# First attention of a three-layer block: heads scored in pairs, one product for the gates' sums

## The chip, the core and the metric

The kernel runs on one core of one Trainium2 chip. A core has five engines that run side by side and wait for each other through semaphores: TensorE (matrix products; PE in the profile, PEld for its weight loads), VectorE (DVE), ScalarE (ACT), GpSimd (POOL) and SyncE (SP, which here starts most transfers). TensorE reads SBUF and writes PSUM, which has eight banks of 128 x 512 floats. The metric is the time of one execution on the device in microseconds (us).

## What is computed

A block of three layers on x of 256 tokens x 1024 channels. The first layer's mixer has a gated short convolution and, beside it, the attention with forget gates that this change is about. In it, eight heads of 64 channels are scored, and the running sums of the logarithms of their gates are added to the scores of the queries and taken from those of the keys:

```python
def forgetting_attention(q, k, v, logf):
    c = jnp.cumsum(logf, axis=1).transpose(0, 2, 1)
    for s0 in range(0, s_len, Q_BLOCK):                       # Q_BLOCK = 128
        logits = jnp.einsum("bqhd,bkhd->bhqk", q[:, s0:s1], k[:, :s1]) * scale
        logits = logits + c[:, :, s0:s1, None] - c[:, :, None, :s1]
        logits = jnp.where(kpos <= qpos, logits, -jnp.inf)
        p = jax.nn.softmax(logits, axis=-1)
        outs.append(jnp.einsum("bhqk,bkhd->bqhd", p, v[:, :s1]))
...
x = x + rmsnorm(mixer(rmsnorm(x)));  x = x + rmsnorm(swiglu(rmsnorm(x)))          # layer 1
# layers 2 and 3: block attention and differential attention, each with a feed-forward;
# their norms are modulated by silu(c) @ ada_w + ada_b (two matrices of 1024 x 6144)
```

## The kernel before

**Slabs.** Every weight comes as a slab of 128 x 2048 floats (1 MB). `load_order` (L88) writes the order of all slabs into STREAM: 160 main slabs in the order of their use, and between them 48 slabs of the modulation (ada). SyncE loads the stream into eight buffers in turn (`raw`, `sp_load` at L478), each as soon as its last user is done. ScalarE rounds a main slab to `high` (L490), VectorE makes the rest `low` (L496), and TensorE multiplies with both. Both engines do this three slabs ahead (AHEAD). An ada slab is used by VectorE alone: two sums of products of 128 x 1024 (L505). Where the ada slabs stand is set by the table `plan`: (count, first slab, last slab) for five stretches; before, 16 stand behind main slabs 4 to 22, and 9 in the first feed-forward.

**Slabs 4 to 14.** `pe_still` (L553) gives a slab of keys, queries, or the mixer's other inputs: 48 products of 256 columns (L569 to L571). Behind each of the slabs 4 to 14 stands one step of the attention, `pe_attend1(n)` with n from 0 to 10. Step n has up to three parts on TensorE: the values of head n-3 (L949, L950), the transposition of the probabilities of head n-2 (L910), and the scores of head n (L844, L962, L963). The scores of a head are, for each of the two query blocks (against 128 and against 256 keys), one product of queries and keys, then two products that take off the keys' sums of log gates, with `ck_hi` and `ck_lo` (the sums rounded, and the rest), each of eight rows, one per head, of which the stationary operand picks one.

**Shapes.** A product is on all 128 rows of the array, or on some: queries and keys of a head lie on 64 partitions (even heads on 0 to 63, odd ones on 64 to 127), the sums on eight. The values of a head have 64 columns of output partitions. The profile shows this as rows*columns ahead of the shape: 128*128, 64*128, 8*128, 128*64.

**VectorE and ScalarE in step n.** VectorE adds the mask and the queries' sums to the scores and finds their maximum (`dve_biased`, L857, L868); ScalarE takes the exponential after the rounding of the next slab (L878); VectorE divides after its next slab (`dve_weigh`, L885, L889); step n+2 transposes. Both engines carry the convolution of the mixer in the same steps. Each engine does its work strictly in the order in which it is written.

**PSUM.** Slabs, transpositions and scores take banks 0 to 3 in turn (`bank`): each waits until what was there is read. Values go to bank 4 + head pair.

The sums of log gates are made once, by L1143 (for the queries) and L1146 (for the keys, negative), from `logf` and `nlogf`, after slab 3; ScalarE copies them to `ck_hi` (L1263), VectorE makes `ck_lo` (L1437), and the first scores wait for that.

Of the kernel before, what the change touches and what calls it, by code (L numbers as in the profile page):

```python
# [12 lines left out]
P = 128  # L13
# [4 lines left out]
H = 8  # L18
# [18 lines left out]
for _name, _n in (("mix_pre", KC), ("ffn_pre", KC), ("conv", 3 * AC), ("subln", 1), ("b_f", NT * H), ("lam", 4 * DIFF)):  # L37
    COLUMNS[_name] = (sum(w for _, w in COLUMNS.values()), _n)
N_COLUMNS = sum(w for _, w in COLUMNS.values())

# [47 lines left out]
def load_order():  # L88

    nets = [(NUM["gate_up1", 0], NUM["moba_v", 0]), (NUM["gate_up2", 0], NUM["diff_v", 0]), (NUM["gate_up2", 2 * FG], len(MAIN))]  # L90
    plan = [(16, 4, 22), (9, nets[0][0] + 4, nets[0][0] + 24), (8, nets[0][1] + 4, nets[1][0] - 2),
# [72 lines left out]
def build_program(nc, dram, out):  # L164
    with ExitStack() as ctx:
# [40 lines left out]
        gate_f = sb("gate_f", [P, 5, NT * H])  # L206
        c_q = sb("c_q", [P, NT * H])
        ck_hi = sb("ck_hi", [H, S], F32R)
        ck_lo = sb("ck_lo", [H, S], F32R)
        ident_r = sb("ident_r", [H, H], F32R)  # L210
# [47 lines left out]
        u_f, a_f, l_f, logf, nlogf = (gate_f[:, i, :] for i in range(5))  # L258
# [572 lines left out]
        def prob_free(tag, h, i):  # L831
            if tag == "s1":
                return (turned, ("s1", h - 4)) if h >= 4 else (small_pe, "gates") if h == 3 else None
# [7 lines left out]
        def pe_scores(tag, h, i, q, k, more=None):  # L841
            o = yield from bank((tag, h, i), (biased, (tag, h, i)))
# [95 lines left out]

        def pe_attend1(n):
            if 0 <= n - 3 < H:  # L940
                h = n - 3
                rows = slice((h % 2) * HD1, (h % 2 + 1) * HD1)
                if h % 2 == 0:
                    yield from bank(("values", "s1", h // 2), *y_bank("s1", h // 2), at=4 + h // 2)
                yield from pe.wait_ge(probs_copied, ("s1", h))
                yield from pe.wait_ge(evacuated, ("values", "v1", 1, 0))
                o, p = psum[4 + h // 2], prob_t[h % 2]
                v = lambda c: work_v[:, c, h * HD1:(h + 1) * HD1]
                nc.tensor.matmul(o[rows, 0:S], v(0), p[:, 0:S], start=True, stop=False)  # L949
                nc.tensor.matmul(o[rows, P:S], v(1), p[:, S:3 * P], start=False, stop=True).then_inc(*applied.up(("s1", h)))  # L950
            if 0 <= n - 2 < H:
                yield from pe_turn_probs("s1", n - 2)
            if n < H:
                h = n
                part = slice((h % 2) * HD1, (h % 2 + 1) * HD1)
                yield from pe.wait_ge(evacuated, ("q1", h // 4))
# [3 lines left out]
                def minus_c(o, w):  # L960
                    row = ident_r[:, h:h + 1].to_broadcast([H, P])
                    nc.tensor.matmul(o, row, ck_hi[:, w], start=False, stop=False)  # L962
                    return nc.tensor.matmul(o, row, ck_lo[:, w], start=False, stop=True)  # L963

                yield from pe_scores("s1", h, 0, qT[part, h // 2, :], kT[part, h // 2, :], minus_c)

        def act_attend1(n):
            if 0 <= n - 3 < H and n % 2 == 0:
                k = (n - 3) // 2
                yield from act_y_hi("s1", k, applied, ("s1", n - 3), psum[4 + k][:, 0:S])  # L970
# [5 lines left out]
        def dve_attend1(n):  # L976
            if 0 <= n - 3 < H and n % 2 == 0:
                yield from dve_y_lo("s1", (n - 3) // 2, psum[4 + (n - 3) // 2][:, 0:S])
# [123 lines left out]
        def tensor():  # L1102
# [42 lines left out]
            for c in range(NT):  # L1145
                m = nc.tensor.matmul(o[0:H, S + c * P:2 * S], nlogf[:, c * H:(c + 1) * H], tri[:, 0:S - c * P],  # L1146
# [73 lines left out]
        def scalar():  # L1220
# [41 lines left out]
            nc.scalar.activation(ident_r[:, :], ident[0:H, 0:H], ACT.Copy)  # L1262
            nc.scalar.activation(ck_hi[:, :], psum[bank_of["sums"]][0:H, S:2 * S], ACT.Copy).then_inc(*small_act.up("ck"))  # L1263
# [16 lines left out]
            for g in range(2):  # L1280
                yield from act_next("mix", g)
# [394 lines left out]
```

## Time and profile before

| | us |
|---|---|
| median of 3 runs (1002.17 to 1004.49) | 1002.32 |
| the profiled execution's own time | 1003.79 |
| its span in the trace | 1002.4 |
| PE busy / DVE busy / ACT busy | 980.0 / 727.0 / 530.8 |
| granted clock of TensorE, mean | 0.995 |

The span runs from the first to the last instruction that the trace shows; the own time holds 1.39 us more. A busy time counts the stretches in which at least one instruction of the engine runs; products overlap, so that a product's duration is longer than the distance to the next. For TensorE the distances between starts are to be read, not the durations.

### The profile page before, as it was taken

To read this page: it belongs to the slowest core of one execution; us is meant where nothing else is said; L and a number is where in the kernel's file an instruction comes from. 1 tells how busy PE (TensorE), PEld (TensorE's weight loads), DVE (VectorE), ACT (ScalarE), POOL (GpSimd) and SP (SyncE) were. 2 spreads that over 40 slices of the span, in tenths; PEclk is the share of its full clock that TensorE was granted. 3 is DMA by queue.
4 is the path that set the end of the run, shared out by engine and by line. 5 is a ranking of instruction groups with operands and counts; after the bars stand their busy time and mean duration, and the time that the engine had idled before them with its cause. 6 is when DMAs were issued, how large, how long until landed. Compare 5 with 4: busy or idle time off the path is not lost.

```text
span 1002.4 us, 14063 instructions
## 1 busy us (share of the span) xinstructions
PE 980.0 (98%) x5762; PEld 856.4 (85%) x5762; DVE 727.0 (73%) x1102; ACT 530.8 (53%) x808; POOL 35.4 (4%) x58
## 2 busy tenths in 40 slices
PE   7999999999999999999999999999999899999997
PEld 7988899878888888899878888887997778888886
DVE  4798867778776777787777878777576768766573
ACT  5644435455444555565564554555567665545451
POOL 2000000011000000000000000001000000000000
PEclk8999999999999999999999999999999999999999
DMA  9665679546997764676467677764733246658511
GB/s 369 263 252 210 235 267 371 219 162 219 241 348 280 271 232 147 218 297 242 168 257 285 259 290 257 288 216 162 229 132 124 85 175 245 216 206 277 205 42 43
DMA packets 33441, 225.67 MB, mean 225 GB/s; under 512 B 4090, under 2 KB 4373, under 8 KB 7008
## 3 DMA queue, kind: packets, MB, share of 16 engines
q1 hardware_dynamic: 31104, 218.94, 60.1%
q0 software_dynamic: 1696, 5.08, 1.6%
q8 instruction: 46, 0.75, 0.3%
q10 hardware_dynamic: 576, 0.74, 0.2%
q14 instruction: 19, 0.16, 0.0%
HBM read 223.49 MB, written 1.26 MB: 224 GB/s over the span
## 4 chain that ended last, share of the span: by engine, by line
PE 85%; DVE 8%; ACT 5%; issue 1%; DMA 1%; POOL 0%; ACTq 0%; DVEq 0%
PE psum L586 20%; PE psum L588 10%; PE psum L625 8%; PE psum L626 8%; PE psum L627 8%; PE psum L569 7%; PE psum L570 7%; PE psum L571 7%; DVE low L496 4%; ACT high L490 2%; PE psum L844 2%; PE psum L694 1%; PE psum L696 1%; PE psum L695 1%; PE psum L311 1%
## 5 line engine op out<-in xcount | busy, mean ns | idle before, releaser
L496 DVE TENSOR_TENSOR low<-raw,high 128x2048 fp32r<-128x2048 f32 (+1 forms) x160 | 361.5, 2276 | 123.2 <-ACT high L490 122.8
L490 ACT ACTIVATE high<-raw 128x2048 fp32r<-128x2048 f32 (+1 forms) x160 | 299.4, 1897 | 36.0 <-DMA raw<-in_mix 9.4
L586 PE MATMUL psum<-h_both,high 128*128 128x512 f32 x960 | 239.9, 392 | 0.0
L586 PEld LDWEIGHTS psum<-h_both,high 128*128 128x128 f32 x960 | 174.3, 189 | 32.9 <-issue 0.5
L569 PE MATMUL psum<-h_both,high 128*128 128x256 f32 x544 | 156.6, 288 | 0.0
L570 PE MATMUL psum<-h_both,high 128*128 128x256 f32 x544 | 153.9, 283 | 0.0
L571 PE MATMUL psum<-h_both,low 128*128 128x256 f32 x544 | 153.9, 283 | 0.0
L588 PEld LDWEIGHTS psum<-h_both,low 128*128 128x128 f32 x960 | 131.0, 190 | 9.4
L588 PE MATMUL psum<-h_both,low 128*128 128x256 f32 x960 | 133.9, 282 | 0.0
L625 PE MATMUL psum<-high,y_hi 128*128 128x512 f32 x328 | 129.2, 394 | 2.6 <-DVE y_lo L932 1.7
L626 PE MATMUL psum<-low,y_hi 128*128 128x512 f32 x328 | 128.0, 390 | 0.0
L627 PE MATMUL psum<-high,y_lo 128*128 128x512 f32 x328 | 127.7, 389 | 0.0
L505 DVE CUSTOM_DVE_ANT_0 raw<-raw,c_row 128x1024 f32<-128x1024 f32 x96 | 113.5, 1220 | 1.0 <-DMA raw<-in_ada 1.0
L595 ACT ACTIVATE work_v<-psum 128x256 f32<-128x256 f32 x120 | 44.0, 376 | 119.6 <-PE psum L588 119.6
L569 PEld LDWEIGHTS psum<-h_both,high 128*128 128x128 f32 x544 | 104.2, 192 | 3.0 <-issue 1.7
L570 PEld LDWEIGHTS psum<-h_both,high 128*128 128x128 f32 x544 | 104.3, 192 | 0.2
L571 PEld LDWEIGHTS psum<-h_both,low 128*128 128x128 f32 x544 | 104.3, 192 | 0.0
L625 PEld LDWEIGHTS psum<-high,y_hi 128*128 128x128 f32 x328 | 61.7, 188 | 15.6 <-DVE low L496 1.9
L627 PEld LDWEIGHTS psum<-high,y_lo 128*128 128x128 f32 x328 | 61.6, 188 | 13.2
L626 PEld LDWEIGHTS psum<-low,y_hi 128*128 128x128 f32 x328 | 61.7, 188 | 11.5
L601 DVE TENSOR_TENSOR work_v<-psum,work_v 128x256 f32<-128x256 f32 x120 | 47.4, 419 | 20.8 <-ACT work_v L595 19.9
L764 ACT ACTIVATE y_hi<-work_v 128x512 fp32r<-128x512 f32 x30 | 19.0, 632 | 62.0 <-DVE work_v L787 62.0
(176 smaller groups left out, 1033.4 us busy)
## 6 DMA issues: line engine op xcount, KB each, us to landing
raw<-in_gate_up SPq DMA_DIRECT2D x66, 1024.0 KB, 5.6
raw<-in_ada SPq DMA_DIRECT2D x48, 1024.0 KB, 4.9
raw<-in_down SPq DMA_DIRECT2D x33, 1024.0 KB, 5.7
raw<-in_mix SPq DMA_DIRECT2D x14, 1024.0 KB, 6.9
raw<-in_moba_qk SPq DMA_DIRECT2D x8, 1024.0 KB, 6.0
raw<-in_diff_qk SPq DMA_DIRECT2D x8, 1024.0 KB, 4.9
raw<-in_qk SPq DMA_DIRECT2D x4, 1024.0 KB, 14.6
raw<-in_branch SPq DMA_DIRECT2D x4, 1024.0 KB, 5.8
```

Source lines behind the costliest of these rows:

```text
L490: nc.scalar.activation(high[n % N_HI][:, s], raw[i % N_RAW][:, s], ACT.Copy).then_inc(*rounded.up(n if key is None else key))
L496: nc.vector.tensor_tensor(low[i % N_RAW][:, s], raw[i % N_RAW][:, s], high[n % N_HI][:, s].bitcast(F32), ALU.subtract).then_inc(*rest.up(key))
L505: last = nc.vector.tensor_tensor_reduce(out=w, in0=w, in1=c_row[:, :], scale=1.0, scalar=0.0, op0=ALU.mult, op1=ALU.add, accum_out=mod_raw ...
L569: nc.tensor.matmul(to, a, hi(k), start=first, stop=False)
L570: nc.tensor.matmul(to, a, lo(k), start=False, stop=False)
L571: m = nc.tensor.matmul(to, r, hi(k), start=False, stop=last and j > j0)
L586: nc.tensor.matmul(o[:, :], wh[:, k, j * P:(j + 1) * P], h_both[:, k, :, :], start=k == 0, stop=False)
L588: m = nc.tensor.matmul(o[:, 0:S], wl[:, k, j * P:(j + 1) * P], h_hi[:, k, :], start=False, stop=k == KC - 1)
L601: nc.vector.tensor_tensor(place[:, j, :], psum[bank_of[*key, j]][:, 0:S], place[:, j, :], ALU.add).then_inc(*joined.up((*key, j)))
L625: nc.tensor.matmul(psum[b][:, :], hi(k0 + k, t), vh, start=first, stop=False)
L626: nc.tensor.matmul(psum[b][:, :], hi(k0 + k, t), vl, start=False, stop=False)
L627: m = nc.tensor.matmul(psum[b][:, :], lo(k0 + k, t), vh, start=False, stop=last)
```

## The change

It does four things. (1) The keys' sums come out of one product on all partitions: `nlogf` is now 128 columns wide with the eight heads at columns 0, 32, 64 and 96, and zeros between them. In the new tile `ck`, rows 0 to 7 and 64 to 71 hold the rounded sums, rows 32 to 39 and 96 to 103 the rest; one product of forty rows (`CK_ROWS`) replaces the two of eight, with a stationary operand (`pick`) that picks the head's row in both groups. (2) Even steps score two heads one behind the other, the odd one into bank 7; odd steps score none. (3) The values of two heads are made one behind the other in even steps from step 4 on. (4) The plan puts 14 ada slabs instead of 16 behind the slabs 4 to 22, and 11 instead of 9 into the first feed-forward. In steps 6 and 7 ScalarE and VectorE do the attention's part ahead of the convolution's last part.

```diff
-    plan = [(16, 4, 22), (9, nets[0][0] + 4, nets[0][0] + 24), (8, nets[0][1] + 4, nets[1][0] - 2),
+    plan = [(14, 4, 22), (11, nets[0][0] + 4, nets[0][0] + 24), (8, nets[0][1] + 4, nets[1][0] - 2),
...
+        nlogf = prob[2][:, 0:NT * P].rearrange("p (t n) -> p t n", t=NT)
...
-        def pe_scores(tag, h, i, q, k, more=None):
-            o = yield from bank((tag, h, i), (biased, (tag, h, i)))
+        def pe_scores(tag, h, i, q, k, more=None, at=None):
+            o = yield from bank((tag, h, i), (biased, (tag, h, i)), at=at)
...
         def pe_attend1(n):
-            if 0 <= n - 3 < H:
-                h = n - 3
...
+            if n % 2 == 0 and 0 <= n - 4 < H:
+                k = (n - 4) // 2
+                o = yield from bank(("values", "s1", k), *y_bank("s1", k), at=4 + k)
                 yield from pe.wait_ge(evacuated, ("values", "v1", 1, 0))
+                for h in (n - 4, n - 3):
+                    rows, p = slice((h % 2) * HD1, (h % 2 + 1) * HD1), prob_t[h % 2]
+                    yield from pe.wait_ge(probs_copied, ("s1", h))
...
-            if n < H:
-                h = n
+            for h in (n, n + 1) if n % 2 == 0 and n < H else ():
                 part = slice((h % 2) * HD1, (h % 2 + 1) * HD1)
+                sums = slice((h % 2) * HD1, (h % 2) * HD1 + CK_ROWS)
...
                 def minus_c(o, w):
-                    row = ident_r[:, h:h + 1].to_broadcast([H, P])
-                    nc.tensor.matmul(o, row, ck_hi[:, w], start=False, stop=False)
-                    return nc.tensor.matmul(o, row, ck_lo[:, w], start=False, stop=True)
-
-                yield from pe_scores("s1", h, 0, qT[part, h // 2, :], kT[part, h // 2, :], minus_c)
+                    return nc.tensor.matmul(o, pick[sums, h:h + 1].to_broadcast([CK_ROWS, P]), ck[sums, w], start=False, stop=True)
+
+                yield from pe_scores("s1", h, 0, qT[part, h // 2, :], kT[part, h // 2, :], minus_c, at=7 if h % 2 else None)
...
-                m = nc.tensor.matmul(o[0:H, S + c * P:2 * S], nlogf[:, c * H:(c + 1) * H], tri[:, 0:S - c * P],
+                m = nc.tensor.matmul(o[:, S + c * P:2 * S], nlogf[:, c, :], tri[:, 0:S - c * P],
...
-            nc.vector.tensor_scalar(nlogf, logf, -1.0, None, ALU.mult).then_inc(*small_dve.up("logf"))
+            yield from dve.wait_ge(small_pool, "blank")
+            for a in range(0, P, 32):
+                m = nc.vector.tensor_scalar(nlogf[:, :, a:a + H], logf.rearrange("p (t h) -> p t h", t=NT), -1.0, None, ALU.mult)
...
-            nc.vector.tensor_tensor(ck_lo[:, :], psum[bank_of["sums"]][0:H, S:2 * S], ck_hi[:, :].bitcast(F32), ALU.subtract).then_inc(
-                *small_dve.up("ck"))
+            for row in (32, 96):
+                rows = slice(row, row + H)
+                m = nc.vector.tensor_tensor(ck[rows, :], psum[bank_of["sums"]][rows, S:2 * S], ck[rows, :].bitcast(F32), ALU.subtract)
+            m.then_inc(*small_dve.up("ck"))
...
+            nc.gpsimd.memset(nlogf, 0.0).then_inc(*small_pool.up("blank"))
```

On TensorE, step 4 (behind slab 8) read before as follows. psum and a number is a bank, prob_t the transposed probabilities, high a rounded slab.

```order
L949 MATMUL psum4<-prob_t1,work_v 64x256 [waits probs_copied]
L950 MATMUL psum4<-prob_t1,work_v 64x128
L910 MATMUL psum3<-const,prob2 128x128 [waits weighted,produced]
L910 MATMUL psum3<-const,prob2 128x128 x2
L844 MATMUL psum0<-work 128x128
L962 MATMUL psum0<-ck_hi,ident_r 128x128
L963 MATMUL psum0<-ck_lo,ident_r 128x128
L844 MATMUL psum0<-work 128x256
L962 MATMUL psum0<-ck_hi,ident_r 128x256
L963 MATMUL psum0<-ck_lo,ident_r 128x256
L569 MATMUL psum1<-h_both,high3 128x256 [waits biased,rest]
```

After the change it reads so (the lines are three further down in the file; two more rows, L847 and L964 of 256 columns into psum7, follow):

```order
L952 MATMUL psum4<-prob_t0,work_v 64x256
L953 MATMUL psum4<-prob_t0,work_v 64x128
L952 MATMUL psum4<-prob_t1,work_v 64x256 [waits probs_copied]
L953 MATMUL psum4<-prob_t1,work_v 64x128
L913 MATMUL psum1<-const,prob2 128x128 [waits weighted,biased]
L913 MATMUL psum1<-const,prob2 128x128 x2
L847 MATMUL psum2<-work 128x128 [waits produced]
L964 MATMUL psum2<-ck,pick 128x128
L847 MATMUL psum2<-work 128x256
L964 MATMUL psum2<-ck,pick 128x256
L847 MATMUL psum7<-work 128x128 [waits biased]
L964 MATMUL psum7<-ck,pick 128x128
```

The values of heads 0 and 1 now stand together, and so do the scores of heads 4 and 5, of which the second waits on its own for bank 7. The products of eight rows are gone. Step 5, behind slab 9, has the transposition alone:

```order
L574 MATMUL psum3<-h_both,low5 128x256
L913 MATMUL psum0<-const,prob3 128x128 [waits weighted,evacuated]
L913 MATMUL psum0<-const,prob3 128x128 x2
L572 MATMUL psum1<-h_both,high4 128x256 [waits probs_copied,rest]
L573 MATMUL psum1<-h_both,high4 128x256
```

It has lost its values and its scores; they stand in steps 6 and 4. On SyncE, in the first feed-forward, before the change:

```order
L484 DMA raw0<-in_down1 128x2048
L484 DMA raw1<-in_ada 128x2048
L484 DMA raw2<-in_gate_up1 128x2048
L484 DMA raw3<-in_gate_up1 128x2048
L484 DMA raw4<-in_ada 128x2048
L484 DMA raw5<-in_down1 128x2048
L484 DMA raw6<-in_gate_up1 128x2048
L484 DMA raw7<-in_gate_up1 128x2048
L484 DMA raw0<-in_ada 128x2048
L484 DMA raw1<-in_down1 128x2048
L484 DMA raw2<-in_gate_up1 128x2048
L484 DMA raw3<-in_ada 128x2048
```

The same place after it:

```order
L487 DMA raw6<-in_down1 128x2048
L487 DMA raw7<-in_ada 128x2048
L487 DMA raw0<-in_gate_up1 128x2048
L487 DMA raw1<-in_gate_up1 128x2048
L487 DMA raw2<-in_ada 128x2048
L487 DMA raw3<-in_down1 128x2048
L487 DMA raw4<-in_gate_up1 128x2048
L487 DMA raw5<-in_ada 128x2048
L487 DMA raw6<-in_gate_up1 128x2048
L487 DMA raw7<-in_down1 128x2048
L487 DMA raw0<-in_ada 128x2048
L487 DMA raw1<-in_gate_up1 128x2048
```

The third ada slab comes one main slab earlier, since eleven now stand where nine stood.

## Rows read from the trace of the kernel before

**Rows 1.** The page: busy time of TensorE; the chain that ended last, by engine.
```profile
PE 980.0 (98%) x5762; PEld 856.4 (85%) x5762; DVE 727.0 (73%) x1102; ACT 530.8 (53%) x808; POOL 35.4 (4%) x58
...
PE 85%; DVE 8%; ACT 5%; issue 1%; DMA 1%; POOL 0%; ACTq 0%; DVEq 0%
```

**Rows 2.** Windows: us, busy time (x instructions) of PE, PEld, DVE, ACT, POOL, clock, DMA share, GB/s.
```profile
44.90:134.60 89.70, 89.70 (x650) 79.46 (x649) 74.80 (x132) 40.42 (x69) 0.00 (x0) 1.00 0.62 234
134.60:180.60 46.00, 46.00 (x384) 46.00 (x384) 34.96 (x37) 20.29 (x15) 0.00 (x0) 1.00 0.84 320
240.00:300.00 60.00, 60.00 (x319) 51.72 (x318) 44.81 (x54) 29.30 (x32) 5.72 (x10) 1.00 0.95 287
```

**Rows 3.** Timeline of PE, the step before slab 9: start us, us, engine, line, tiles, shape.
```profile
83.32 0.28 PE L571 MATMUL psum<-h_both,low 128*128 128x256 f32 x1
83.53 0.65 PE L949 MATMUL psum<-prob_t,work_v 128*64 128x256 f32 x2
84.01 0.38 PE L950 MATMUL psum<-prob_t,work_v 128*64 128x128 f32 x2
84.33 0.55 PE L910 MATMUL psum<-const,prob 128*128 128x128 f32 x3
84.80 0.48 PE L844 MATMUL psum<-work 64*128 64x128 f32 x2
85.22 0.32 PE L962 MATMUL psum<-ck_hi,ident_r 8*128 8x128 f32 x1
85.58 0.70 PE L844 MATMUL psum<-work 64*128 64x256 f32 x2
86.20 0.38 PE L962 MATMUL psum<-ck_hi,ident_r 8*128 8x256 f32 x1
86.43 0.28 PE L963 MATMUL psum<-ck_lo,ident_r 8*128 8x256 f32 x1
86.64 0.38 PE L569 MATMUL psum<-h_both,high 128*128 128x256 f32 x1
```

**Rows 4.** Timeline of PE, first product of slabs 4, 5, 6, 7, 8 and 15.
```profile
44.90 0.39 PE L569 MATMUL psum<-h_both,high 128*128 128x256 f32 x1
...
52.67 0.38 PE L569 MATMUL psum<-h_both,high 128*128 128x256 f32 x1
...
60.44 0.39 PE L569 MATMUL psum<-h_both,high 128*128 128x256 f32 x1
...
68.55 0.38 PE L569 MATMUL psum<-h_both,high 128*128 128x256 f32 x1
...
77.59 0.39 PE L569 MATMUL psum<-h_both,high 128*128 128x256 f32 x1
...
134.55 0.39 PE L569 MATMUL psum<-h_both,high 128*128 128x256 f32 x1
```

**Rows 5.** Timeline of PE, third attention, both halves of a head.
```profile
722.58 0.28 PE L571 MATMUL psum<-h_both,low 128*128 128x256 f32 x1
722.78 0.93 PE L844 MATMUL psum<-work 64*128 64x128 f32 x8
723.65 0.38 PE L569 MATMUL psum<-h_both,high 128*128 128x256 f32 x1
```

**Rows 6.** Timeline of DVE, then of PE, around the first score.
```profile
49.87 0.41 DVE L1437 TENSOR_TENSOR ck_lo<-psum,ck_hi 8x256 fp32r<-8x256 f32 x1 [0.54 <-ACT ck_hi L1263]
...
50.84 0.48 PE L844 MATMUL psum<-work 64*128 64x128 f32 x2
```

**Rows 7.** Timeline of DVE: a score's bias, with the wait before it.
```profile
77.70 0.74 DVE L857 SCALAR_TENSOR_TENSOR prob<-psum,c_q,const 128x128 f32<-128x128 f32 x2 [2.41 <-PE psum L963]
```

**Rows 8.** Timeline of DVE, then of PE: one slab of the first feed-forward.
```profile
288.61 2.29 DVE L496 TENSOR_TENSOR low<-raw,high 128x2048 fp32r<-128x2048 f32 x1 [1.02 <-ACT high L490]
...
298.00 0.63 PE L586 MATMUL psum<-h_both,high 128*128 128x512 f32 x2
```

**Rows 9.** The page, groups of instructions: busy us, mean ns; idle before, its releaser.
```profile
L505 DVE CUSTOM_DVE_ANT_0 raw<-raw,c_row 128x1024 f32<-128x1024 f32 x96 | 113.5, 1220 | 1.0 <-DMA raw<-in_ada 1.0
```

More of the change, by code:

```diff
@@ L257, in build_program @@
         table, hot = prob[0][0:BUCKETS + 1, 0:H * COPIES], prob[1][0:BUCKETS + 1, :]
-        u_f, a_f, l_f, logf, nlogf = (gate_f[:, i, :] for i in range(5))
+        u_f, a_f, l_f, logf = (gate_f[:, i, :] for i in range(4))
+        nlogf = prob[2][:, 0:NT * P].rearrange("p (t n) -> p t n", t=NT)
         def col(name, a=0, n=None):
@@ L832, in prob_free @@
             if tag == "s1":
[L833 removed]
+                return (turned, ("s1", h - 4)) if h >= 4 else (None, None, (small_pe, "sums"), (small_pe, "gates"))[h]
             if tag == "moba":
@@ L939, in pe_attend1 @@
         def pe_attend1(n):
-            if 0 <= n - 3 < H:
-                h = n - 3
[L942 to L945, printed above, removed]
-                yield from pe.wait_ge(evacuated, ("values", "v1", 1, 0))
[L947 to L950, printed above, removed]
+            if n % 2 == 0 and 0 <= n - 4 < H:
+                k = (n - 4) // 2
+                o = yield from bank(("values", "s1", k), *y_bank("s1", k), at=4 + k)
+                yield from pe.wait_ge(evacuated, ("values", "v1", 1, 0))
+                for h in (n - 4, n - 3):
+                    rows, p = slice((h % 2) * HD1, (h % 2 + 1) * HD1), prob_t[h % 2]
+                    yield from pe.wait_ge(probs_copied, ("s1", h))
+                    v = lambda c: work_v[:, c, h * HD1:(h + 1) * HD1]
+                    nc.tensor.matmul(o[rows, 0:S], v(0), p[:, 0:S], start=True, stop=False)
+                    nc.tensor.matmul(o[rows, P:S], v(1), p[:, S:3 * P], start=False, stop=True).then_inc(*applied.up(("s1", h)))
             if 0 <= n - 2 < H:
                 yield from pe_turn_probs("s1", n - 2)
-            if n < H:
-                h = n
+            for h in (n, n + 1) if n % 2 == 0 and n < H else ():
                 part = slice((h % 2) * HD1, (h % 2 + 1) * HD1)
+                sums = slice((h % 2) * HD1, (h % 2) * HD1 + CK_ROWS)
                 yield from pe.wait_ge(evacuated, ("q1", h // 4))
@@ L976, in dve_attend1 @@
         def dve_attend1(n):
-            if 0 <= n - 3 < H and n % 2 == 0:
-                yield from dve_y_lo("s1", (n - 3) // 2, psum[4 + (n - 3) // 2][:, 0:S])
+            if n % 2 == 0 and 0 <= n - 4 < H:
+                yield from dve_y_lo("s1", (n - 4) // 2, psum[4 + (n - 4) // 2][:, 0:S])
             if n < H:
@@ L1281, in scalar @@
                 yield from act_next("mix", g)
+                yield from act_attend1(6 + g)
                 yield from act.wait_ge(produced, ("conv", g))
@@ L1284, in scalar @@
                     *hi_made.up(("conv", g)))
-                yield from act_attend1(6 + g)
             for n, place in enumerate((gate_c, gate_a)):
@@ L1467, in vector @@
                     *produced.up(("conv", g)))
+                yield from dve_attend1(6 + g)
                 yield from dve.wait_ge(hi_made, ("conv", g))
@@ L1470, in vector @@
                     *lo_made.up(("conv", g)))
-                yield from dve_attend1(6 + g)
             for n in range(2):
@@ L1641 @@
         "lam": np.broadcast_to(a["diff_lambda_2"][0].reshape(1, -1), (P, 4 * DIFF)),
+        "pick": (row % 32 == np.arange(H)[None, :]).astype(np.float32),
     }
```

19 lines of the change are left out of this document (10 added, 9 removed).

## The prediction

> **What bounds the kernel now.** I read the page first, then the chain of waits, the windows of the attention, TensorE's timeline within one step, and last VectorE's timeline. The page shows TensorE busy for 980.0 us and on 85% of the chain that ended last, the other engines on 8% or less [rows 1]. In the window of steps 0 to 10, from slab 4 to slab 15, it is busy for all of 89.70 us, VectorE for 74.80 and ScalarE for 40.42 [rows 2]. So time saved on TensorE there ends the stretch earlier, as long as VectorE keeps up.
>
> The reader is to see in the next rows where TensorE's time goes though it looks busy. In the window without attention (134.6 to 180.6) 384 products of slabs take 46.00 us [rows 2], so 0.12 us each and 48 x 0.12 = 5.75 us a slab. Slab 4 begins at 44.90 and slab 15 at 134.55 [rows 4]: 89.65 us for eleven slabs (63.25) and eleven steps, which leaves 26.4 us for the attention. Step 0 is scores alone: 52.67 - 44.90 - 5.75 = 2.02 us. Step 2 is scores and a transposition: 68.55 - 60.44 - 5.75 = 2.36, so a transposition costs 0.34. Step 4 (slab 8 begins at 77.59, slab 9 at 86.64 [rows 3, 4]) has values too: 3.30, so values cost 0.94. Eight of each: 16.2 + 2.7 + 7.5 = 26.4, as measured.
>
> Most of a head's 2.02 us is no streaming. At each change of the rows or columns in use the next start is 0.2 us away: the slab's last product at 83.32, the values at 83.53; the sums' last product at 86.43, the next slab at 86.64 [rows 3]. Within a slab the distance is 0.12. A switch thus costs some 0.09 ahead of the new shape and as much behind it, where its first weights load uncovered. The scores of a head change shape five times: 128 to 64 rows, to 8 (85.22), to 64 (85.58), to 8 (86.20), to 128 (86.64).
>
> The nearest thing to the new pair stands in the third attention, where the two halves of a head lie on partitions 0 to 63 and 64 to 127, go to two banks, and have no product for sums between. Their eight records take from 722.78 to 723.65 [rows 5], 0.87 us. One after the other they could not: a 128-key record streams in about 0.11 (three transpositions in 0.34) and a 256-key one in 0.21 (0.48 from 83.53 to 84.01 for two, less the first load [rows 3]), which makes 4 x 0.11 + 4 x 0.21 = 1.28 without any load or switch. So the two halves run side by side although the program has one half behind the other. TensorE: Matmul & The Clock Gate, in the Trainium skill (Part 3, The mechanism), says that products start and end strictly in program order. By it the second head's streaming would come behind the first's; the trace disagrees, with 0.87 against at least 1.28, and its rule is rival B below.
>
> **The change part by part.**
>
> *Scores.* If forty rows count as the same half of the array as sixty-four, a pair is one visit: 0.09 + 0.87 + 0.09 = 1.05 us for queries and keys, plus two products for the sums per head, side by side with the other head's. Each costs at least nothing (under a load) and at most 0.36, what the two products and their switch take now (85.22 to 85.58 [rows 3]). I take 0.12 each, as a slab's product, since it has the same columns: 1.05 + 0.24 = 1.29. Before, two heads cost 2 x 2.02 = 4.04. Saved: 4 x 2.75 = 11.0 us. With the sums' products free it is 12.0.
>
> *Values.* Eight visits of 0.94 become four. If two heads on different columns run side by side too, a visit stays at 0.96, and 7.5 - 3.8 = 3.7 us go. No row shows two products on different columns at a time. If they don't, the second head adds its streaming, some 0.65 of the 0.80 between 83.53 and 84.33 [rows 3]: 4 x 1.59 = 6.4, and 1.2 us go. I take the first, because the rows of the array do it. TensorEngine Tiling (Array Packing), in the Trainium skill (Key Properties), says that tiles work independently and in parallel; by it too the saving would be 3.7, and no run here shows it for columns.
>
> *Transpositions.* As many as before, 0.34 each; in odd steps they stand between slabs of their own shape. Nothing.
>
> *Making the sums.* Once: four products with 128 stationary columns instead of eight. Four longer loads against two switches that go: between 0.2 us gained and 0.2 lost; taken at nothing. On VectorE `ck` needs a second subtraction, 0.41 long, behind one that starts at 49.87, so it is ready at about 50.65 instead of 50.28; the first score starts at 50.84 [rows 6]. That is a cover of 0.2 us; if it fails I lose 0.1 to 0.3. The three more negations, some 0.17 each by the smallest VectorE work here, and GpSimd's clearing of `nlogf` at the very start are ahead of a slab's worth of time; nothing.
>
> *VectorE.* Its work in the stretch is 74.80 us and its room falls from 89.7 to 75.0. It gets one ada slab less there (two sums of 1.22 [rows 9]) and 0.6 us of new work: 73 of 75. That is close, and it is the cover on which everything hangs. What keeps it from the path: it is ahead today, waiting 2.41 us for the scores of head 3 [rows 7], a rest is made three slabs ahead, and a division has a whole slab of 5.75 us until its transposition. An even step now waits for the odd head's bias two slabs before. Queued behind such a wait are the pair's scores and the next slab. I put 0.3 us for it, and 3 at worst.
>
> *Loads.* Two ada slabs move into the first feed-forward, where the DMA engines are busy for 95% of the time at 287 GB/s [rows 2], so 3.7 us per slab. A rest there ends at 290.90 and its slab starts at about 298.0 [rows 8], 7.1 us ahead. One or two slabs more in front of it leave 3.4 us or just nothing; the cost is between 0 and 2 us, taken at 0. In the first stage there are two slabs fewer in less time.
>
> Sum: -11.0 - 3.7 + 0.3 = -14.4 us. Against the profiled execution's own 1003.79 us that gives 989.4. It was 1.47 above the median of the runs, so the median should come to 987.9, say 988.0.
>
> **The rivals.**
>
> A. *Columns one after the other.* The values save 1.2 instead of 3.7: 11.0 + 1.2 - 0.3 = 11.9, 990.4 us. For it: no row shows columns together, and both heads write one bank. Against it: the rows do.
>
> B. *Heads in program order.* The second head's scores stream behind the first's: 0.64 + 0.24 = 0.88 more for a pair, 7.5 us saved instead of 11.0, and the values as in A: 993.9 (with the values side by side 991.4). Against it: [rows 5].
>
> C. *The cover fails in part.* VectorE at 73 of 75 us is late for banks or divisions, or the feed-forward's slabs come late: 1 to 3 us back, 989 to 991.
>
> D. *Forty rows are a shape of their own.* Then each head keeps its five switches and the halves can't overlap. Per head only two products of about 0.06 and 0.12 go, and per pair one switch to and from: 4 x (0.36 + 0.18) = 2.2, with the values' 3.7 less 0.3: 996.8. Against it: a head's array rows come in halves in every row that I have, and forty fit the half; but no row shows forty.
>
> E. *Slower, by VectorE.* In each of the four even steps with scores TensorE stands until VectorE has read the odd head's scores of two steps before. That costs nothing until VectorE is more than a slab late. It loses when the stand is over 3.6 us a step (14.4 / 4), and over 0.3% slower from 4.4 us a step: 1006 or more. For it: 97% load. Against it: VectorE's own work doesn't grow, and before it fitted with 14.9 us to spare.
>
> **How the numbers follow.** The forecast (986.5 to 989.5) has 0.50, A 0.20, C 0.14, B 0.08, D 0.05, E 0.03. The low end is the forecast with the sums' products free and 0.2 gained in making the sums, with some spread of the runs: 986.0. The high end takes in A, C and B's better half: 992.5. Left out are most of B, D and E above, and little below. A measurement of this kernel can't tell less than 0.3% (3 us) from no change; all cases but E are beyond that, with D nearest. So 0.95 faster, 0.02 the same, 0.03 slower.
>
> **What would show it.** On TensorE's timeline a pair's twelve records must begin within about 0.9 us, with distances of 0.01 to 0.02 between the two heads, and the next slab start 1.1 after the first. The even step from 4 on must take about 2.6 us, odd ones 0.34, and the stretch from slab 4 to slab 15 about 75. Gaps of 0.2 around the products of `ck` would be D, the second head's records behind the first's B, the same at L952 A. Waits of TensorE for VectorE in the stretch (there are none now) would be C or E. The forecast is wrong if the stretch shrinks by less than 12 us, or if it does and the end comes later by less: then the feed-forward has eaten it.

## The result and the profile after

| | before | after |
|---|---|---|
| median (4 runs each, one comparison) | 1002.25 (1001.91 to 1004.49) | 990.01 (989.59 to 990.60) |
| profiled execution's own time / span | 1003.79 / 1002.4 | 989.94 / 988.6 |
| slab 4 to slab 15 | 89.65 | 76.37 |

The ratio is 0.9873, 95% interval 0.9861 to 0.9885: faster by 1.3%, 12.2 us between the medians. The forecast was 988.0 us in a range of 986.0 to 992.5. The page of the changed kernel, busy time and chain by engine:

```profile
PE 966.1 (98%) x5746; PEld 849.7 (86%) x5746; DVE 727.4 (74%) x1106; ACT 531.0 (54%) x808; POOL 35.7 (4%) x59
...
PE 83%; DVE 9%; ACT 5%; issue 1%; DMA 1%; POOL 0%; ACTq 0%; DVEq 0%
```

TensorE is busy 13.9 us less than in [rows 1], the other engines as long as before. The windows that answer to [rows 2] (the attention, the slabs without it, the feed-forward):

```profile
44.41:120.81 76.40, 76.25 (x636) 72.77 (x634) 72.68 (x129) 40.49 (x69) 0.00 (x0) 1.00 0.69 261
120.81:166.86 46.05, 46.05 (x386) 46.05 (x385) 32.69 (x32) 20.27 (x15) 0.00 (x0) 1.00 0.79 298
226.20:286.20 60.00, 60.00 (x319) 51.72 (x318) 46.85 (x60) 29.09 (x32) 5.72 (x10) 1.00 0.97 304
```

The attention's window is 13.3 us shorter (it starts 0.03 ahead of slab 4's first product; the expectations below give the stretch as its 76.40), TensorE is busy in nearly all of it, and VectorE does nearly its old work in less room. The next two windows are full, as before. Behind the start of slab 15 the two executions take the same, 1002.4 - 134.55 = 867.85 us and 988.6 - 120.81 = 867.79: nothing was given back. The timeline of PE, first products of slabs 4, 5, 7, 8, 9 and 15, beside [rows 4]:

```profile
44.44 0.36 PE L572 MATMUL psum<-h_both,high 128*128 128x256 f32 x1
...
51.97 0.39 PE L572 MATMUL psum<-h_both,high 128*128 128x256 f32 x1
...
65.42 0.38 PE L572 MATMUL psum<-h_both,high 128*128 128x256 f32 x1
...
71.52 0.36 PE L572 MATMUL psum<-h_both,high 128*128 128x256 f32 x1
...
80.14 0.38 PE L572 MATMUL psum<-h_both,high 128*128 128x256 f32 x1
...
120.81 0.39 PE L572 MATMUL psum<-h_both,high 128*128 128x256 f32 x1
```

Less 5.75 us a slab, step 0 is 51.97 - 44.44 - 5.75 = 1.78 us (forecast 1.29) and step 2, behind an empty step 1, 65.42 - 51.97 - 11.5 = 1.95 (forecast 1.63). Step 3, a transposition alone, is 71.52 - 65.42 - 5.75 = 0.35, and step 4 is 80.14 - 71.52 - 5.75 = 2.87 (forecast 2.6). The timeline of PE in step 4 answers to [rows 3]:

```profile
77.45 0.66 PE L952 MATMUL psum<-prob_t,work_v 128*64 128x256 f32 x4
77.93 0.40 PE L953 MATMUL psum<-prob_t,work_v 128*64 128x128 f32 x4
78.25 0.55 PE L913 MATMUL psum<-const,prob 128*128 128x128 f32 x3
78.73 0.49 PE L847 MATMUL psum<-work 64*128 64x128 f32 x2
78.97 0.30 PE L964 MATMUL psum<-ck,pick 40*128 40x128 f32 x1
79.06 0.48 PE L847 MATMUL psum<-work 64*128 64x128 f32 x3
...
79.41 0.46 PE L964 MATMUL psum<-ck,pick 40*128 40x256 f32 x1
...
79.74 0.47 PE L964 MATMUL psum<-ck,pick 40*128 40x256 f32 x1
```

Three things are to be seen. The values of two heads, twice the records, take from 77.45 to 78.25, the 0.80 that one head took from 83.53 to 84.33 [rows 3]. At the sums' product there is no gap: the first head's records start at 78.73, 78.94, 78.97 (the sums) and 79.12. And the second head of the pair starts at 79.06, 0.33 behind the first (78.73), while the next slab starts 1.41 behind it; 1.1 was forecast. In step 0 one more thing stands on the same timeline, and on that of DVE:

```profile
50.16 0.28 PE L574 MATMUL psum<-h_both,low 128*128 128x256 f32 x1
50.59 0.46 PE L847 MATMUL psum<-work 64*128 64x128 f32 x2 [0.15 <-DVE ck L1443]
```

```profile
49.58 0.86 DVE L1443 TENSOR_TENSOR ck<-psum,ck 8x256 fp32r<-8x256 f32 x2 [0.55 <-ACT ck L1264]
```

The scores start 0.43 behind the slab's last product, where a switch takes 0.21. They wait for the two subtractions of `ck`, which end at 50.44, and start 0.15 behind that end.

### The profile page after: what moved, and what is told of

Same layout as the page of the kernel before. It is cut to its first block, busy times and chain, and to the rows that moved or that the text cites. A ratio compares the mean times of both kernels' runs of the same rounds, so it can differ in the third digit from the quotient of the medians.

```text
span 988.6 us, 14035 instructions
## 1 busy us (share of the span) xinstructions
PE 966.1 (98%) x5746; PEld 849.7 (86%) x5746; DVE 727.4 (74%) x1106; ACT 531.0 (54%) x808; POOL 35.7 (4%) x59
## 3 DMA queue, kind: packets, MB, share of 16 engines
HBM read 223.49 MB, written 1.26 MB: 227 GB/s over the span
## 4 chain that ended last, share of the span: by engine, by line
PE 83%; DVE 9%; ACT 5%; issue 1%; DMA 1%; POOL 0%; ACTq 0%; DVEq 0%
PE psum L589 20%; PE psum L591 10%; PE psum L628 8%; PE psum L629 8%; PE psum L630 8%; PE psum L572 7%; PE psum L574 6%; PE psum L573 6%; DVE low L499 4%; ACT high L493 2%; PE psum L847 1%; PE psum L697 1%; PE psum L698 1%; PE psum L699 1%; PE psum L314 1%
## 5 line engine op out<-in xcount | busy, mean ns | idle before, releaser
L630 PEld LDWEIGHTS psum<-high,y_lo 128*128 128x128 f32 x328 | 61.6, 188 | 13.2
L629 PEld LDWEIGHTS psum<-low,y_hi 128*128 128x128 f32 x328 | 61.7, 188 | 11.5
```

What stands on the lines that cost most here:

```text
L629: nc.tensor.matmul(psum[b][:, :], hi(k0 + k, t), vl, start=False, stop=False)
L630: m = nc.tensor.matmul(psum[b][:, :], lo(k0 + k, t), vh, start=False, stop=last)
```

## The experiments

Two theories on the late head. A head's scores are six records (two of L847, one of L964, and the same with 256 columns), so the odd head's first is the seventh of the pair; it starts at 79.06. The even head's sixth, its last, starts only at 79.41. The timeline of PEld shows what else goes at 79.06:

```profile
78.73 0.29 PEld L847 LDWEIGHTS psum<-work 64*128 64x128 f32 x2 [0.17 <-issue]
...
79.06 0.30 PEld L847 LDWEIGHTS psum<-work 64*128 64x128 f32 x4
```

Four weight loads of L847 take there what two take at 78.73: the odd head's first load goes together with the even head's fourth. One theory: TensorE takes up only what stands a few records ahead of what it runs. The rival: the odd head is held by the forty rows or by its own wait for bank 7 (`at=7`, `biased`).

**The two heads in turn.** In the scores' step, head after head becomes product after product:

```diff
-            for h in (n, n + 1) if n % 2 == 0 and n < H else ():
-                yield from pe_scores("s1", h, 0, ..., minus_c, at=7 if h % 2 else None)
+                for t, w in enumerate((W0, W1)):
+                    for h, o in zip((n, n + 1), both):
+                        nc.tensor.matmul(o[:, w], qT[part, h // 2, tile_of(t)], kT[part, h // 2, keys], start=True, stop=False)
+                    for h, o in zip((n, n + 1), both):
+                        m = nc.tensor.matmul(o[:, w], pick[sums, h:h + 1]..., ck[sums, keys], start=False, stop=True)
```

> Changed kernel, but the two heads of a pair are written product by product in turn (queries and keys of both for the first block, sums of both, then the second block). In the changed kernel the odd head's first record starts 0.33 us behind the even one's. Theory W (TensorE looks only a few products ahead, and the odd head's first is the seventh record): the two heads start 0.01 us apart, a pair is 0.3 us shorter, the stretch from slab 4 to slab 15 falls from 76.4 to about 75.2 us and the time from 990.0 to about 988.9. Rival S (the odd head is held by its own semaphore wait or by the product of forty rows): the distance stays at 0.3 us and the time at 990.0.

Measured: 987.99 us (987.11 to 989.02), ratio to before 0.9849 (0.9834 to 0.9863). The scores of its step 4 on the timeline of PE, and the next slab:

```profile
78.21 0.49 PE L967 MATMUL psum<-work 64*128 64x128 f32 x4
78.46 0.31 PE L970 MATMUL psum<-ck,pick 40*128 40x128 f32 x2
78.60 0.65 PE L967 MATMUL psum<-work 64*128 64x256 f32 x4
78.89 0.47 PE L970 MATMUL psum<-ck,pick 40*128 40x256 f32 x2
79.30 0.39 PE L572 MATMUL psum<-h_both,high 128*128 128x256 f32 x1
```

From the first score to the next slab 79.30 - 78.21 = 1.09 in place of 1.41, with the same products and banks. Both waits for banks now stand ahead of the first product; the second kernel below has that alone. The steps are now 1.62 (step 2) and 2.55 (step 4), near the forecast's 1.63 and 2.6. So the order in which the products stand costs the 0.33 us. The median is 2.0 us below the changed kernel's; the stretch is 75.18, 1.2 shorter, as expected, and the rest lies outside it.

**Sums last; waits first.** Two kernels that leave the order of the heads. In the first the forty-row products of a head stand behind both its products of keys; in the second the odd head's bank is waited for ahead of the even head's products.

```diff
+                for t, w in enumerate((W0, W1)):
+                    nc.tensor.matmul(o[:, w], qT[...], kT[...], start=t == 0, stop=False)
+                for t, w in enumerate((W0, W1)):
+                    m = nc.tensor.matmul(o[:, w], pick[...], ck[...], start=False, stop=t == 1)
```

```diff
+                if h % 2 == 0:
+                    for b in (h, h + 1):
+                        yield from bank(("s1", b, 0), (biased, ("s1", b, 0)), at=7 if b % 2 else None)
```

> Changed kernel, but each head's four products are queries and keys of both blocks, then the sums of both blocks; the odd head still comes behind the even one. Theory W (odd head's first record is the seventh, and comes into view when the third or fourth of the even head starts): the fourth record is now the second pass of 256 keys, which starts later (at 0.43 instead of 0.33 us), so the odd head starts 0.2 to 0.45 us behind, not sooner than 0.2. Rival F (the product of forty rows just ahead of the second block holds what follows): the distance falls to 0.01 or 0.02 us.

> Changed kernel with the heads one behind the other as there, but both waits for banks ahead of the even head's products, so that the odd head's first weight load carries none. Theory W (a look-ahead of a few products): the odd head's first record still starts 0.33 us behind the even one's, and steps 2 and 4 stay at 1.96 and 2.89 us. Rival S (its own wait holds it): 0.01 us, and 1.63 and 2.57 us as with the heads in turn.

Measured: 990.52 and 992.44 us, one execution each, and the steps of the changed kernel but for step 0 (1.90 in the second). With waits first the odd head again starts 0.33 behind (78.73 and 79.06):

```profile
78.73 0.49 PE L971 MATMUL psum<-work 64*128 64x128 f32 x2
78.98 0.30 PE L964 MATMUL psum<-ck,pick 40*128 40x128 f32 x1
79.06 0.49 PE L971 MATMUL psum<-work 64*128 64x128 f32 x3
```

Neither the head's wait nor the place of the forty rows makes it late. With the sums last it starts at 78.51, again 0.33 behind (78.18). The even head's fourth product moves there from 0.39 to 0.54 us behind its first, its fourth weight load stays at 0.33, and the odd head's first load again goes with it. What is left is that it stands six records behind. Two behind (the heads in turn) or four behind (the values here, the halves in [rows 5]) is in time. That a limited look-ahead does this is inferred from these cases; nothing in the trace shows it directly. The second kernel's longer time isn't in the attention. The waits of PE (us in total, times, longest) in that kernel, then in the changed one:

```profile
PE psum L628 <- DVE y_lo L794: 2.7, 2, 2.3
```

```profile
PE psum L628 <- DVE y_lo L794: 0.7, 2, 0.4
```

2.0 of its 2.5 us stand there, far from the edit, in one execution.

**One subtraction for `ck`.** Over all partitions, with a column that is -1 where the rounded sums are to be taken off:

```diff
-            for row in (32, 96):
-                rows = slice(row, row + H)
-                m = nc.vector.tensor_tensor(ck[rows, :], psum[...][rows, S:2 * S], ck[rows, :]..., ALU.subtract)
+            nc.vector.scalar_tensor_tensor(out=ck[:, :], in0=ck[:, :]..., scalar=col("is_lo"), in1=psum[...][:, S:2 * S],
+                                           op0=ALU.mult, op1=ALU.add)
```

> Changed kernel, but the rest of the sums is made by one VectorE instruction on all partitions instead of two on eight rows each. TensorE waited 0.2 us for the second one before its first score. Theory: the wait goes and step 0 takes 1.6 instead of 1.8 us; the time falls by 0.2 us, to 989.8, which the runs can hardly tell. Rival: VectorE's later work comes 0.3 us earlier too and the time falls by 0.5 us or more.

Measured: 989.48 us (989.28 to 990.38), 0.9865 (0.985 to 0.988). Step 0 falls from 1.78 to 1.59, the wait is gone, the others stay, and the stretch is 0.20 us shorter, as the theory had it. The median is 0.5 below the changed kernel's, the rival's number, but the 0.3 us more don't lie in the stretch, and runs of one kernel scatter by more than that.

**The plan of the loads as before.**

```diff
-    plan = [(14, 4, 22), (11, nets[0][0] + 4, nets[0][0] + 24), ...
+    plan = [(16, 4, 22), (9, nets[0][0] + 4, nets[0][0] + 24), ...
```

> Changed kernel with the old plan of the modulation's slabs (16 behind slabs 4 to 22, 9 in the first feed-forward). Theory C of the prediction (VectorE's room is the cover, and two slabs fewer keep it): VectorE has 2.4 us more work in a stretch of 76.4 us in which it is busy for some 73, so TensorE waits 0.5 to 3 us and the time is 990.5 to 993. Rival: where the two slabs stand is hidden anyway, VectorE's work is ahead by several us at every step, and the time stays at 990.0 within 0.3.

Measured: 989.87 us (989.33 to 990.36), 0.9867 (0.985 to 0.9883); every step as in the changed kernel. VectorE now works 72.97 of 75.90 us in the attention (44.90 to 120.80), and TensorE still waits for it only the 0.2 us for `ck`. So the two slabs may stand in either stage, and VectorE at 96% holds nothing up. The new order of ScalarE's and VectorE's work in steps 6 and 7 is in every version here; no run shows what it is worth.

**A transposition between the two heads.**

```diff
-            if 0 <= n - 2 < H:
+            if 0 <= n - 2 < H and (n % 2 or n >= H):
                 yield from pe_turn_probs("s1", n - 2)
...
+                if h % 2 == 0 and 0 <= n - 2 < H:
+                    yield from pe_turn_probs("s1", n - 2)
```

> Changed kernel, but in steps 2, 4 and 6 the transposition of 128 rows stands between the scores of the even and of the odd head, so that they can't run side by side. Theory H (the halves' overlap is worth a head's streaming): a head alone takes 1.05 us and a switch each way 0.18, so a pair costs 2.46 instead of 1.6, 0.87 more in three steps: the time is 990.0 + 2.6 = 992.6. Rival (only switches count): 0.18 more per step, 990.5.

Measured: 993.37 us (991.76 to 994.23), 0.99 (0.9885 to 0.9915). Steps 2, 4 and 6 are 2.84, 3.61 and 3.62, so 2.4 us more over three steps (2.6 expected). The median rose by 3.4; in the profiled execution slab 4 begins 1.0 us later than in the changed kernel's, ahead of anything that this edit touches. The timeline of PE in step 4:

```profile
80.09 0.48 PE L847 MATMUL psum<-work 64*128 64x128 f32 x2
...
81.16 0.55 PE L913 MATMUL psum<-const,prob 128*128 128x128 f32 x3
81.64 0.49 PE L847 MATMUL psum<-work 64*128 64x128 f32 x2
```

A head alone takes 81.16 - 80.09 = 1.07 us; in e1_interleaved two take 1.09. A transposition uses all rows and closes the overlap.

**Forty rows, one head a step.** The scores of head n in step n, the values still in pairs:

```diff
-            for h in (n, n + 1) if n % 2 == 0 and n < H else ():
+            for h in (n,) if n < H else ():
```

> Changed kernel with the product of forty rows, but one head's scores in every step as before the change (values still in pairs). Theory H: a head alone is 1.05 us between switches of 0.18, so 1.23 instead of 2.02 before; two of them cost 2.46 against 1.6 to 1.96 for the pair, so the stretch is 4 x 0.5 = 2.0 us (step 0: 0.65) longer than the changed kernel's 76.4, and the time 992.2. By it the forty rows alone are worth 8 x 0.79 = 6.3 us and the pairing some 2.2 to 3.5. Rival (the pair is worth more than the forty rows): over 995.

Measured: 994.60 us (993.70 to 995.61), 0.9914 (0.9897 to 0.9931). The stretch is 80.08, step 1 is 1.28: one head alone, beside 2.02 before. The expected 2.0 us more were too few, since the text above let a pair cost up to 1.96, which holds a transposition; a pair is 1.62 (0.21 from the slab's last product to its first, and 1.41), so pairing is worth 2 x 1.28 - 1.62 = 0.94 us, four times, and the stretch is 3.7 us longer.

The even head's keys and its sums stand on the same half of the rows, before and here; the odd head's sums stood before on rows 0 to 7, away from its keys. Yet steps 0 and 1 of the kernel before, an even and an odd head, take 2.02 each [rows 4]. So what a head alone gains comes with forty rows instead of eight and not with the new place.

**Pairs, with two products of eight rows.** Pairs of scores and of values as in the change, the sums as before it:

```diff
-                    return nc.tensor.matmul(o, pick[sums, h:h + 1]..., ck[sums, w], start=False, stop=True)
+                    row = pick[0:H, h:h + 1].to_broadcast([H, P])
+                    nc.tensor.matmul(o, row, ck[0:H, w], start=False, stop=False)
+                    return nc.tensor.matmul(o, row, ck_lo[:, w], start=False, stop=True)
```

> Changed kernel (pairs in even steps, values in pairs), but with the sums of the keys taken off by two products of eight rows as before the change. Theory H: with eight rows each head changes shape five times and nothing overlaps, so a pair costs 2 x 1.84 + 0.18 = 3.86 us instead of 1.6 to 1.8; the stretch grows by 4 x 2.2 = 8.9 us and the time from 990.0 to 998.9. Rival (the pairing brings most, the switches are hidden by the other head): less than 994.

Measured: 1003.43 us (1000.77 to 1009.32, 10 runs), ratio 1.0014 (0.9994 to 1.0034): no gain at all. A pair costs 3.85, as expected: in step 0 the even head's last product starts at 52.01, the odd head's first at 52.21. The heads follow one another. Here both heads' sums stand on rows 0 to 7; whether pairs could overlap with eight rows in each head's own half, no run shows. But the stretch is 89.62 us. By its steps, where the clock stood, it would be 85.2 (3.85 + 4.19 + 2 x 5.11 + 3 x 0.35 + 1.29 + 0.33 + 0.98 = 21.9, and 63.25 for the slabs). PE's timeline behind step 2, then its windows of 2 us (the clock is the third number from the end):

```profile
69.53 0.28 PE L967 MATMUL psum<-ck_lo,pick 8*128 8x256 f32 x1
70.12 0.41 PE L574 MATMUL psum<-h_both,high 128*128 128x256 f32 x1
...
70.75 0.42 PE L574 MATMUL psum<-h_both,high 128*128 128x256 f32 x1
```

```profile
70.00:72.00 2.00, 2.00 (x10) 2.00 (x11) 2.00 (x5) 0.43 (x2) 0.00 (x0) 0.50 1.03 434
72.00:74.00 2.00, 2.00 (x15) 2.00 (x14) 1.97 (x2) 0.00 (x0) 0.00 (x0) 0.71 0.20 82
...
104.00:106.00 2.00, 2.00 (x6) 1.13 (x5) 1.97 (x7) 2.00 (x2) 0.00 (x0) 0.50 0.99 414
106.00:108.00 2.00, 2.00 (x10) 1.88 (x10) 2.00 (x4) 1.15 (x5) 0.00 (x0) 0.50 0.52 217
```

The granted clock falls to 0.50, the level of 1.2 GHz, and the slab's products are 0.21 us apart instead of 0.12. Neither kernel of the comparison shows that in the attention. Was it an accident?

> e7_two_products once more, unchanged, for a second profile. There a pair cost 3.87 us as expected, but the granted clock stood at about 0.7 in the windows after steps 2 and 6 (68 to 72 us, 102 to 112 us), which made the stretch from slab 4 to slab 15 some 4.4 us longer than its steps. If the dense visits of small products bring the clock down, it falls in steps 2 to 6 again, slabs there show products 0.2 us apart instead of 0.12 for a while, and the stretch is again 88 to 91 us for 85.3 by its steps. Rival (an accident of that one execution, as the lower clock of the first 32 us comes and goes): clock 1.00 in the whole stretch, 85.3 us, and a time near 998 to 999 us.

The same kernel once more took 1004.20 us, with the stretch at 91.05. Windows of PE from it:

```profile
52.00:54.00 2.00, 2.00 (x6) 1.24 (x7) 2.00 (x3) 0.56 (x1) 0.00 (x0) 0.56 0.98 401
54.00:56.00 2.00, 2.00 (x12) 2.00 (x11) 1.97 (x4) 0.99 (x4) 0.00 (x0) 0.50 1.01 426
```

The clock fell again, this time during step 0, and later behind steps 2 and 4. So it is no accident; in which steps it falls changes, which goes with the wide spread of the runs (8.6 us). Their mean clocks over the whole execution agree: 0.983 to 0.993 in the ten runs, beside 0.992 to 0.998 in the thirteen runs of the kernel before that were taken with them. That the dense visits of small products cause it is the likeliest reading, since they are the main thing in which this kernel differs from the changed one. What exactly sets it off stays open.

**The values apart.** The scores in pairs, each head's values in a step of its own as before:

```diff
-            if n % 2 == 0 and 0 <= n - 4 < H:
-                for h in (n - 4, n - 3):
+            if 0 <= n - 3 < H:
+                h = n - 3
```

> The changed kernel with the values as before: each head's two products of the values in a step of its own (after slabs 3 + h), none beside another head's; the scores stay in pairs with the forty rows. Theory (the pairing of the values is worth 0.94 us a pair, since the visit of a head is 0.93 to 0.95 us by the change of array mode and the four products, and the second head's runs beside it for nothing): 4 x 0.94 = 3.8 us more, odd steps 5 to 11 at 1.27 in place of 0.33, stretch 80.1 to 80.2 us in place of 76.40, median 993.6 to 993.9 us. Rival (the time of a visit lies in the waits beside it and not in the products; a lone visit in a step without scores costs little): odd steps at 0.6 to 0.8, stretch 77.5 to 78.3, median 991 to 992 us.

Measured: 993.58 us (993.25 to 994.21), 0.9905 (0.9889 to 0.9922); odd steps from 3 on at 1.29, stretch 80.07: 3.7 us more. Its visit of one head, 79.34 - 78.55 = 0.79, is as long as the visit of two above:

```profile
78.55 0.65 PE L953 MATMUL psum<-prob_t,work_v 128*64 128x256 f32 x2
79.03 0.38 PE L954 MATMUL psum<-prob_t,work_v 128*64 128x128 f32 x2
79.34 0.55 PE L913 MATMUL psum<-const,prob 128*128 128x128 f32 x3
```

**Both small costs away.** The heads in turn and the single subtraction together (the two diffs above).

> The two heads' products written in turn (as in e1_interleaved) and ck by one subtraction over all partitions (as in e2_one_subtraction), together. If the two costs of the change are separate, the late head's 0.33 us in each of four steps and the 0.2 us wait for ck in step 0, both are gone: step 0 1.29 us in place of 1.81, steps 4 and 6 2.57 for 2.89, the stretch from slab 4 to slab 15 75.0 us in place of 76.40 (1.4 less), and the median 988.3 to 988.8 us by what the stretch alone gives, 987.7 to 988.3 if e1_interleaved's 2.0 us below the changed kernel repeat. Rival: the heads of e1_interleaved are together because step 0 is late anyway, or the single subtraction, which runs over 128 partitions, comes no earlier than the second of the two: then step 0 stays at 1.5 to 1.6 and the stretch at 75.2 to 75.3.

Measured: 989.47 us (988.31 to 990.63), 0.9864 (0.9849 to 0.9878). PE's timeline, slab 4, the scores of step 0, and slab 15:

```profile
43.95 0.36 PE L572 MATMUL psum<-h_both,high 128*128 128x256 f32 x1
...
49.67 0.28 PE L574 MATMUL psum<-h_both,low 128*128 128x256 f32 x1
49.88 0.49 PE L967 MATMUL psum<-work 64*128 64x128 f32 x4
...
118.79 0.39 PE L572 MATMUL psum<-h_both,high 128*128 128x256 f32 x1
```

The switch takes its 0.21 again, step 0 is 1.26, and the stretch is 74.84 us, 1.5 less than in the changed kernel: the two costs are separate, and together they are what the forecast of the stretch missed. The median doesn't follow: it is 0.5 below the changed kernel's and 1.5 above that of the heads in turn alone. By the stretch this version is the best, by the runs it isn't told apart from its neighbours.

**The kernel before, once more.**

> The kernel before, profiled once more and unchanged, to see how far one profiled execution lies from the median and in which part of the program. The prediction took the profiled run's 1003.79 us as 1.47 above the median and carried that over to the changed kernel. If the first 32 us and the waits of the last third scatter from run to run (slab 2 began at 30.1 to 32.5 us in the eight profiles so far), the stretch from slab 4 to slab 15 is 89.6 to 89.7 us here too, and the time anywhere from 1001.5 to 1004.3 us. Rival (the offset belongs to the profiling of the kernel before): 1003.5 to 1004.1 again, with the same waits at the same places.

Measured: 1001.59 us. Its windows row for the first 32 us, after the same row of the first profile:

```profile
0.00:32.00 32.00, 26.72 (x139) 23.29 (x140) 19.27 (x33) 17.16 (x30) 7.08 (x13) 0.89 0.95 380
```

```profile
0.00:32.00 32.00, 26.59 (x160) 22.59 (x161) 19.95 (x34) 19.66 (x32) 8.33 (x13) 1.00 0.96 380
```

The timeline of PE, slabs 4 and 15 in this one:

```profile
42.38 0.39 PE L569 MATMUL psum<-h_both,high 128*128 128x256 f32 x1
...
132.03 0.39 PE L569 MATMUL psum<-h_both,high 128*128 128x256 f32 x1
```

The stretch is 89.65, to the hundredth as in [rows 4]. Slab 4 begins 2.5 us earlier, where the clock stays at 1.00 in the first 32 us instead of 0.89. All fourteen profiles of this case fall in with that: slab 4 begins at 44.3 to 45.4 us in the nine with 0.89 there, at 43.0 to 44.0 in the four with 0.95, and at 42.4 in this one. So executions scatter ahead of the attention, and a single one, or a median of four, can be 1 us off either way. The two profiles of the comparison both have 0.89.

## Why the prediction was right, and where it was off

**The bound.** Right: TensorE's time in the attention was the time. 13.3 of the 13.85 us between the two profiled executions lie in the stretch and 0.5 ahead of slab 4. Of these 0.5 some 0.17 are the making of the sums, which the forecast took at nothing: from the first product of the sums to slab 4 it takes 1.24 us instead of 1.41. The rest is in the range in which executions scatter.

**Scores.** The mechanism was right, the size too large: 11.0 us forecast, 2.42 x 4 = 9.7 measured. The failed term is the pair, 1.62 and not 1.29 us. I took the row of the third attention, where the second half stands four records behind the first, and left out that here the second head stands six behind. With the heads in turn and `ck` in time the pair is 1.26 us (step 0 of the last version). That it comes so near the term is in part luck, since the 0.12 us for each product of the sums was a choice between 0 and 0.36. The split: forty rows instead of two times eight are worth 8 x (2.02 - 1.28) = 5.9 us, the overlap 3.7. The first also goes ahead of the second: with the two products of eight rows as they stood, pairing the scores saves only 4 x (4.04 - 3.85) = 0.8 us.

**Values.** Right: 3.7 forecast, 3.7 measured in e6_values_apart. Products on different columns run side by side. TensorEngine Tiling (Array Packing), in the Trainium skill (Key Properties), says so too, and the trace agrees, with 0.80 us for two heads and 0.79 for one. TensorE: Matmul & The Clock Gate, in the Trainium skill (Part 3, The mechanism), says that products start and end in program order. Between products on different halves of the rows the runs here disagree. In the changed kernel the odd head's first product starts at 79.06, 0.35 us ahead of the even head's last (79.41), which stands before it in the program. That the heads' products follow one another, which rival B took from it, the runs refute too, with 1.09 us for a pair against 1.07 for a head.

**`ck`.** The cover of 0.2 us didn't hold. The first subtraction begins 5.14 us behind slab 4's start (49.58 - 44.44) and not 4.97 (49.87 - 44.90 [rows 4, 6]), and the two take 0.86. The sum of the cover also left out the 0.15 us from the end of the second to the start of the waiting product. Cost 0.2, in the bounds given (0.1 to 0.3).

**VectorE and loads.** 0.3 us were put down for VectorE: none came. It works 72.7 us in the stretch (forecast 73), and the only wait of TensorE for it there is that for `ck`. In the feed-forward a rest ends at 277.55 and its slab starts at 284.23, 6.7 us ahead instead of 7.1 [rows 8]:

```profile
275.27 2.28 DVE L499 TENSOR_TENSOR low<-raw,high 128x2048 fp32r<-128x2048 f32 x1
```

```profile
284.23 1.09 PE L589 MATMUL psum<-h_both,high 128*128 128x512 f32 x4
```

**The sum.** -9.7 - 3.7 + 0.2 = -13.2 us against 14.4 forecast; the stretch shows -13.3, and 0.2 more went in the making of the sums. Carried to the median, 1.47 us were taken off, the distance of one execution from a median of three. The 31 timed runs of the kernel before, in four comparisons, have a median of 1003.0, 0.8 below that execution, and 1003.0 - 13.4 = 989.6, with 990.01 measured. So of the 2.0 us between forecast and result 1.0 are the sum's, and the rest is the carrying and the scatter of medians. Against the four runs of its own comparison the gain is only 12.2 us. The two profiles, with the same clock in the first 32 us, don't show where 1 us more could be lost; I put it down to the few runs, and that is not shown.

**The rivals.** The result lies 0.5 above the forecast's own range, near the times of A (990.4) and C (989 to 991), but by neither's mechanism: columns run together, and no cover but that of `ck` failed. The sign that the forecast named, a stretch shorter by less than 12 us, didn't come either: it is 13.3 shorter. B and D are refuted by the pair's records, E by the absent waits. A time near a rival's proves nothing for it; the rows decide.

## What to carry to other kernels

Count the changes of row group and column group in a stretch of small products: here each costs about 0.09 us on either side (0.21 from start to start instead of 0.12), and a term padded to the neighbours' group (forty rows in place of two times eight) was worth more than the pairing of the scores behind it (5.9 and 3.7 us). Work that is to overlap on different rows is best written in turn, product by product, with nothing of the whole array in between; six records behind cost 0.33 us here, two or four cost nothing. Judge edits worth 1 us by the stretch in the trace and not by medians of four runs.

## What was not expected of the hardware

- A second head six records behind the first starts 0.33 us late though its rows are free, with the first head's fourth weight load; four or two records behind, it starts with the first. In both cases it starts ahead of products that stand before it in the program.
- Two heads on different columns, writing the same bank, take as long as one: 0.80 us for eight records, 0.79 for four.
- In the kernel with dense products of eight rows TensorE's clock falls to 1.2 GHz in the middle of a full stretch, in both profiles, for 4.5 and 5.9 us of loss (89.62 and 91.05 against 85.2 by its steps). In the two profiles of the kernel before, where the small products are spread over all steps, it stays at 1.00 there.
